# Where TensorE's operands stand in SBUF: the attention and FFN activations and the normalised input are given other byte addresses

## The reference

```
for i in range(DEPTH):                     # 4
    x = x + 0.5 * rmsnorm(swiglu(rmsnorm(x, g[0]), wg1[i], wu1[i], wd1[i]), g[1])
    xn = rmsnorm(x, g[2])
    y = conv_mixer | dilated_attention | mlstm | conv_mixer     # layers 0, 1, 2, 3
    x = x + rmsnorm(y, g[3])
    x = x + 0.5 * rmsnorm(swiglu(rmsnorm(x, g[4]), wg2[i], wu2[i], wd2[i]), g[5])
swiglu(x, wg, wu, wd) = (silu(x @ wg) * (x @ wu)) @ wd          # 1024 -> 2816 -> 1024
```

## The kernel before, in words

| tensor | before | modulo 256 |
|---|---|---|
| w_high, w_low | 25728, 74880 | 128 |
| xT_high, xT_low | 148800, 156992 | 64 |
| oT_hi, oT_lo | 212448, 220640 | 224 |

## Time and profile before

### The profile page before, as it was taken

One profiled execution on the slowest core, in us unless ns is written; L12 is line 12 of the kernel. 1 busy time (PEld: TensorE's weight loads), 2 busy tenths in 40 slices (PEclk: granted clock), 3 DMA queues, 4 the chain that ended last, 5 costly groups with the idle time before them and its releaser, 6 DMA issues.

```text
span 2140.2 us, 35887 instructions
## 1 busy us (share of the span) xinstructions
PE 2108.0 (98%) x14636; PEld 1931.7 (90%) x14636; DVE 1185.7 (55%) x1346; ACT 965.4 (45%) x1177; POOL 52.5 (2%) x100
## 2 busy tenths in 40 slices
PE   8999999999998999999999999999999999999998
PEld 6998989988998998997999899898999899898997
DVE  5555765456456554555645654555645654576543
ACT  5444544344435544454444543554444543544442
POOL 0000000000000000000000000000000000000000
PEclk9999999999999999999999999999999999999999
DMA  8554655546554342342644545453644555455551
GB/s 317 185 191 167 221 185 203 206 160 216 194 185 172 124 153 100 119 158 94 232 186 179 206 187 203 153 193 134 231 185 178 205 188 203 154 212 187 205 187 60
DMA packets 55981, 386.27 MB, mean 180 GB/s; under 512 B 6592, under 2 KB 7104, under 8 KB 10816
## 3 DMA queue, kind: packets, MB, share of 16 engines
q1 hardware_dynamic: 52416, 372.53, 47.2%
q10 hardware_dynamic: 3456, 12.13, 1.6%
HBM read 383.58 MB, written 1.05 MB: 180 GB/s over the span
## 4 chain that ended last, share of the span: by engine, by line
PE 98%; ACT 1%; DVE 0%; issue 0%; DMA 0%; POOL 0%; POOLq 0%; ACTq 0%; DVEq 0%
PE ps L407 29%; PE ps L409 29%; PE ps L408 29%; PE ps L420 2%; PE ps L423 2%; PE ps L426 2%; PE ps L687 1%; PE ps L712 1%; PE ps L700 1%; PE ps L442 1%; PE ps L689 0%; PE ps L674 0%; PE ps L714 0%; ACT xT_high L905 0%; PE ps L497 0%
## 5 line engine op out<-in xcount | busy, mean ns | idle before, releaser
L1219 DVE TENSOR_TENSOR w_low<-raw,w_high 128x2048 fp32r<-128x2048 f32 x352 | 804.2, 2289 | 321.3 <-ACT w_high L881 321.1
L407 PE MATMUL ps<-xT_high,w_high 128*128 128x256 f32 x2656 | 736.0, 277 | 0.0
L409 PE MATMUL ps<-xT_high,w_low 128*128 128x256 f32 x2656 | 734.9, 277 | 0.0
L408 PE MATMUL ps<-xT_low,w_high 128*128 128x256 f32 x2656 | 734.5, 277 | 0.0
L881 ACT ACTIVATE w_high<-raw 128x2048 fp32r<-128x2048 f32 x352 | 670.7, 1911 | 37.7 <-DMA raw<-stream 21.1
L408 PEld LDWEIGHTS ps<-xT_low,w_high 128*128 128x128 f32 x2656 | 499.4, 188 | 2.7
L407 PEld LDWEIGHTS ps<-xT_high,w_high 128*128 128x128 f32 x2656 | 499.0, 188 | 3.1
L409 PEld LDWEIGHTS ps<-xT_high,w_low 128*128 128x128 f32 x2656 | 498.6, 188 | 0.0
L916 ACT ACTIVATE region<-ps 128x256 f32<-128x256 f32 x176 | 67.6, 384 | 668.6 <-PE ps L409 651.3
L407 PE MATMUL ps<-w_high,oT_hi 128*128 128x512 f32 x832 | 330.4, 397 | 0.0
L409 PE MATMUL ps<-w_high,oT_lo 128*128 128x512 f32 x832 | 329.6, 396 | 0.0
(11 more groups left out here) (147 smaller groups left out, 1258.3 us busy)
## 6 DMA issues: line engine op xcount, KB each, us to landing
raw<-stream SPq DMA_DIRECT2D x352, 1024.0 KB, 4.8
gain<-gains ACTq DMA_DIRECT2D x23, 512.0 KB, 4.7
x<-x_in SPq DMA_DIRECT2D x2, 512.0 KB, 6.0
out<-x SPq DMA_DIRECT2D x2, 512.0 KB, 2.6
gain<-gains SPq DMA_DIRECT2D x1, 512.0 KB, 5.3
att_mask<-att_mask_in SPq DMA_DIRECT2D x1, 384.0 KB, 5.1
rope<-rope_in SPq DMA_DIRECT2D x1, 128.0 KB, 4.5
ml_mask<-ml_mask_in SPq DMA_DIRECT2D x1, 128.0 KB, 4.9
```

Of the source, the lines that this page charges most:

```text
L407: nc.tensor.matmul(acc, lh, rh, start=start, stop=False)
L408: nc.tensor.matmul(acc, lh, rl, start=False, stop=False)
L409: return nc.tensor.matmul(acc, ll, rh, start=False, stop=stop)
L1219: nc.vector.tensor_tensor(w_low[:, p % RING, :], raw[:, p % RAW, :], w_high[:, p % RING, :], ALU.subtract).then_inc(piece_split, 1)
```

## The change

The tensors change place; no instruction is added, removed or moved, and no wait is changed. `oT_hi` and `oT_lo` are allocated directly behind the weight rings. `xT_high` and `xT_low` become two views of one tensor `xT_both`, which has 240 floats of room; each of the twelve sublayers shifts the views by its entry of `PLACE` (floats). To make room the table `rope` moves into the unused end of `region`, which shrinks from 9900 to 9872 floats.

```diff
-REGION = 9900
+REGION = 9872
+ROPE_AT = 9400
+PLACES = 240
+PLACE = (0, 224, 64, 0, 224, 128, 0, 224, 192, 0, 32, 0)
...
+        oT_hi = sb("oT_hi", [P, KD, SEQ], F32R)
+        oT_lo = sb("oT_lo", [P, KD, SEQ], F32R)
         x = sb("x", [P, TILES, D])
...
-        xT_high = sb("xT_high", [P, KD, SEQ], F32R)
-        xT_low = sb("xT_low", [P, KD, SEQ], F32R)
+        xT_both = sb("xT_both", [P, 2 * KD * SEQ + PLACES], F32R)
+        sub_now = [0]
+        def xT_view(which):
+            at = PLACE[sub_now[0]] + which * KD * SEQ
+            return xT_both[:, at:at + KD * SEQ].rearrange("p (k c) -> p k c", k=KD)
+        def xT_high():
+            return xT_view(0)
+        def xT_low():
+            return xT_view(1)
...
-        rope = sb("rope", [P, TILES, 2, QH * ROT])
+        rope = region[:, ROPE_AT:ROPE_AT + TILES * 2 * QH * ROT].rearrange("p (t e c) -> p t e c", t=TILES, e=2)
...
-        oT_hi = sb("oT_hi", [P, KD, SEQ], F32R)
-        oT_lo = sb("oT_lo", [P, KD, SEQ], F32R)
...
             for sub, kind in enumerate(KINDS):
+                sub_now[0] = sub
                 program[kind](sub)
```

More of the change, by code:

```diff
@@ L419, in arriving @@
                 for k, cols in rows:
-                    nc.tensor.matmul(acc, xT_high[:, k, tok], w_high[:, slot, cols], start=k == 0, stop=False)
+                    nc.tensor.matmul(acc, xT_high()[:, k, tok], w_high[:, slot, cols], start=k == 0, stop=False)
                 x_ready(joint, t, half)
                 for k, cols in rows:
-                    nc.tensor.matmul(acc, xT_low[:, k, tok], w_high[:, slot, cols], start=False, stop=False)
+                    nc.tensor.matmul(acc, xT_low()[:, k, tok], w_high[:, slot, cols], start=False, stop=False)
                 weights_ready(p)
                 for k, cols in rows:
-                    last = nc.tensor.matmul(acc, xT_high[:, k, tok], w_low[:, slot, cols], start=False, stop=k == KD - 1)
+                    last = nc.tensor.matmul(acc, xT_high()[:, k, tok], w_low[:, slot, cols], start=False, stop=k == KD - 1)
                 return last
@@ L470, in early_block @@
                             cols = slice((k - 4 * half) * 512, (k - 4 * half + 1) * 512)
-                            last = products(ps[:, GU_BANK + i % 2, :], xT_high[:, k, tok], xT_low[:, k, tok],
+                            last = products(ps[:, GU_BANK + i % 2, :], xT_high()[:, k, tok], xT_low()[:, k, tok],
                                             w_high[:, slot, cols], w_low[:, slot, cols], k == 0, k == KD - 1)
@@ L487, in block @@
                             last = products(ps[:, GU_BANK + i % 2, e * SEQ:(e + 1) * SEQ], w_high[:, p % RING, cols],
-                                            w_low[:, p % RING, cols], xT_high[:, k, :], xT_low[:, k, :],
+                                            w_low[:, p % RING, cols], xT_high()[:, k, :], xT_low()[:, k, :],
                                             k == 0, k == KD - 1)
@@ L582, in features_first @@
                         last = products(ps[:, bank, j * SEQ:(j + 1) * SEQ], w_high[:, slot, cols],
-                                        w_low[:, slot, cols], xT_high[:, k, :], xT_low[:, k, :],
+                                        w_low[:, slot, cols], xT_high()[:, k, :], xT_low()[:, k, :],
                                         k == 0, k == KD - 1)
@@ L590, in tokens_first @@
                     tok, cols = slice(t * P, (t + 1) * P), slice(k * 256, (k + 1) * 256)
-                    last = products(acc, xT_high[:, k, tok], xT_low[:, k, tok], w_high[:, slot, cols],
+                    last = products(acc, xT_high()[:, k, tok], xT_low()[:, k, tok], w_high[:, slot, cols],
                                     w_low[:, slot, cols], k == 0, k == KD - 1)
@@ L752, in mlstm @@
                 for k in range(KD):
-                    last = products(ps[0:2 * NH, 2, 0:SEQ], gw_high[:, k, :], gw_low[:, k, :], xT_high[:, k, :],
-                                    xT_low[:, k, :], k == 0, k == KD - 1)
+                    last = products(ps[0:2 * NH, 2, 0:SEQ], gw_high[:, k, :], gw_low[:, k, :], xT_high()[:, k, :],
+                                    xT_low()[:, k, :], k == 0, k == KD - 1)
                 last.then_inc(gates_in_psum, 1)
@@ L904, in xT @@
                     act.wait_ge(xT_in_psum, 4 * joint + 2 * t + b + 1)
-                    nc.scalar.activation(xT_high[:, 4 * b:4 * b + 4, t * P:(t + 1) * P],
+                    nc.scalar.activation(xT_high()[:, 4 * b:4 * b + 4, t * P:(t + 1) * P],
                                          ps[:, xT_bank(joint, t, b), :].rearrange("p (k c) -> p k c", k=4),
@@ L1247, in xT @@
                     cols = slice(t * P, (t + 1) * P)
-                    nc.vector.tensor_tensor(xT_low[:, 4 * b:4 * b + 4, cols],
+                    nc.vector.tensor_tensor(xT_low()[:, 4 * b:4 * b + 4, cols],
                                             ps[:, xT_bank(joint, t, b), :].rearrange("p (k c) -> p k c", k=4),
-                                            xT_high[:, 4 * b:4 * b + 4, cols], ALU.subtract).then_inc(xT_split, 1)
+                                            xT_high()[:, 4 * b:4 * b + 4, cols], ALU.subtract).then_inc(xT_split, 1)
             def times_up(sub, i, turn=0):
```

## The result

The changed kernel takes 2146.6 us (median of nine runs, 2144.96 to 2147.8) against 2140.56 us before (nine runs): a ratio of 1.0025, 95% interval 1.0016 to 1.0035. It is a little slower. The forecast was 2109 us, range 2094 to 2138. The profiled execution has a span of 2144.7 us, from its first to its last instruction; the time of that same execution is 2146.6 us. Every other run here also has a time 1.7 to 1.9 us above its span, so the profiled execution of the kernel before, with a span of 2140.2 us, was one of about 2142 us and not the median one. The spans are 4.5 us apart, the medians 6.0.

The account below looks back on a forecast made before the run. PE was taken to bound the kernel, its time being matmul count times pitch plus joints. From 2140.2 us, -24.2 (D), -0.6 (crossings) and -6.0 (mixers) sum to -30.8, giving 2109 us, range 2094 to 2138.

Parts of the forecast that it names:

- PE bounds the kernel, and addresses act on the pitch: Whole kernel: time is matmul count times start-to-start distance, plus joints; addresses change only how long an access takes.
- Rival 3: Whole kernel: addresses don't matter, or not in this way; time stays at 2140 us (2136 to 2144); chance 0.09.
- Its own time is the span, 2140.2 us: Profiled run of the kernel before: its span equals the median to 0.1 us, so span differences are median differences.
- oT behind the rings: 2496 D matmuls (512 columns): operand distance goes from 160 to 0, pitch from 234.2 to 224.5 ns, 24.2 us less.
- smooth ring: D matmuls: on a ring of 256 bytes, distance 0 lies between free 192 and mild 64, away from bad 96 and 160.
- floor, 220.0 ns: D matmuls: lower bound on pitch if nothing holds them up, 113.3 + 106.7 ns, a gain of 35.4 us.
- The crossings F to D: Eight FFNs, some 64 crossings: distance goes from 96 to 192, 10 ns less each, 0.6 us less.
- xT in the mixers: Mixers: T from 117.7 to 113.3 ns, 10.6 us less; F from 113.3 to 117.7, 4.6 us more; net 6.0 less.
- Nothing else: FFNs and the rest: F and E keep their pitch, since shifts there are multiples of 256 bytes; nothing in the sum.
- Rival 4: D matmuls: distance 0 is the worst case, pitch 240 ns, 2148 us; chance 0.11 together with every other slower way.
- The clock: Two half-clock stretches at the attention may come, go or move: nothing in the sum, 3 us in the range.

Follow-up runs that it names:

- e9_dist64_xT: Changed kernel with oT at remainder 64 modulo 256 bytes instead of 128, no extra matmuls: 2124.12 us, ratio 0.9913 against the kernel before.
- e8_nudge_all: Changed kernel plus one extra 16-column matmul behind every D group that F follows, in all eight FFNs: 2126.07 us, ratio 0.9923 against the kernel before.
- e5_nudge: Changed kernel plus one extra matmul behind each D group that F follows, except the first; another width (16 to 256 columns) per FFN: 2131.86 us, one run.
- e11_before_nudge: Kernel before, addresses untouched, plus one extra matmul behind each D group, the first included; another width (16 to 256 columns) per FFN: 2156.38 us, one run.

## Why the prediction was wrong, point by point

- *PE bounds the kernel, and addresses act on the pitch.* Right. Rival 3, that addresses don't matter, is out: padding alone moved the time to 2131 (one run), and D's pitch with it, and `e9_dist64_xT` is clear of noise at 0.9913. "SBUF — State Buffer" of the Trainium skill, section "Who interferes with whom", has PE never waiting on anyone; D between 226.7 and 234.3 ns by nothing but the place of oT differs from that, and the measurement decides.
- *"Its own time is the span, 2140.2 us"*. A wrong reading: that execution took about 2142 us, and the span agrees with the median only by chance. The forecast hardly depends on it.
- *"oT behind the rings": 224.5 ns, 24.2 us less.* Right in kind, too large. D settles at 226.7, inside the 222 to 228 that the forecast gave itself, and gave 17.5 us. The 224.5 was the middle between two bounds, so that it came near is partly luck. The reason that I gave is not good, though. The picture of a smooth ring, with 0 mild because it lies between 192 and 64, is wrong: 4 bytes off, D is at 233.3, and at 192, which I took for free, also. What I took for a floor, 220.0 ns, was seen at no distance.
- *The crossings F to D*: 0.6 us less. They went from 123 to 118 ns, 0.3 us, since F ahead of them is at 117.8.
- *"xT in the mixers": net 6.0 us less.* T gave 6.3 instead of 10.6: in the attention it went from 117.8 to 114.0, as 57 of its 60 runs settle at 113.3 and the others at 117.8, but mLSTM and the convs gave only 1.0 us together, and T in the second conv nothing. F there cost 1.7 us instead of 4.6, all of it in the first conv: the second was at 117.8 already and mLSTM did not move. So T and F did not trade places, as the sum had them do; net 4.6 instead of 6.0.
- ***"Nothing else. In the FFNs the shifts are multiples of 256 bytes, so F (6912 of 7968 matmuls) and E stay."*** This is the step that failed. E stayed at 228.9. F in the FFNs, put at nothing in the sum, went from 113.6 to 117.5 on average and took 26.9 us more, over all distances. Without it the two spans would differ by 22.7 us in the forecast's direction, some 2118 us; with it the kernel is slower. The third sublayers, shifted by 256, 512 and 768 bytes, show the same F as the others, so it isn't a longer period. Behind D at 226.7 F settles in its slower rhythm; the entry tests show that it is the entry and not the address: one small matmul between the two gives 113.3 (`e8_nudge_all`, and six of eight widths in `e5_nudge`), and in the kernel before the other two widths, 64 and 96, take 113.3 away from every second run (`e11_before_nudge`).
- *The rows had it.* I read F's pitch from one mixer and took it for the kind's. The same run in the second conv, at 117.8, contradicts that a pitch belongs to addresses. It was the exception, too: in the fourteen kernels the two convs have 28 long F runs, and only three of them, one in the kernel before, are at 113.3. And the slow matmuls behind D in the earlier trace rows (118.3 although the distance was right) can be read as F beginning in the slow rhythm and leaving it after five matmuls, which in the changed kernel it does not; that is a reading, not a test.
- *Rival 4* forecast the right sign by a wrong road: D at distance 0 is its fastest, not its slowest.
- *The clock* played a small part: the mean granted clock is 0.997 in both, but 27 T matmuls of the attention fall in the stretches at the lower level and 18 did before, at about 213 ns instead of 113, some 0.9 us. T's 6.3 us are net of it.

Left open: what in the hardware makes the rhythms. That they belong to the stream meeting the next weight load is likely, as the distance between just these two matters, but no run took the loads away, and none kept the other engines' accesses apart from them. Nor do I know why the width of a nudge decides as it does, or why F at 117.8 doesn't leave that rhythm in 377 matmuls.

## What to carry to other kernels

In a stream of matmuls read the pitch, start to start, of every long run of a kind and compare repeats of the same code before tying it to shape or address: two values for one code mean that something other than shape and address decides, here what runs ahead, and then a change to one stage can cost or give in the next. Try operand places as a scan, one offset per repetition within one run, and judge each place by the pitch of its neighbours too. Where a run sits in the slow rhythm, one tiny matmul ahead of it (0.11 us) can be worth more than it costs, but whether it does is to be measured at each place.

## What the runs showed of the hardware that I had not expected

- Long runs of reduced-precision float32 matmuls settle at repeated pitches, most often 113.3, 117.8 or 120.0 ns for 256 columns and 226.7, 228.9 or 233.3 for 512, at the upper clock level. Two of them can exist for the same instructions and addresses (F at distance 192 in the two conv mixers of the kernel before, 113.3 and 117.8), and two for one distance at 512 columns as well (D at 64, 228.9 and 233.3).
- The place of the stationary against the moving operand modulo 256 bytes is worth up to 6% of a matmul of 256 columns (113.3 to 120.0) and 3% of one of 512 (226.7 to 234.3), and shifts of 4 to 16 bytes matter (D at 0, 4 and 16: 226.7, 233.3 and 226.7).
- The same distance is the best for 512 columns and among the worst for 256: at 0, 226.7 and 120.0 ns.
